# The last expert block summed by one-hot products, and the combination and norm put behind the expert loop without a barrier

## Chip, cores and metric

The kernel runs on one core of one Trainium2 chip. The metric is the device time in microseconds (us) of one execution; below, "span" is the time from the first to the last instruction in a profiled execution. The engines are TensorE (PE; its weight loads are shown as PEld), VectorE (DVE), ScalarE (ACT), GpSimd (POOL) and SyncE (SP), which issues most of the DMAs.

## Reference

Two transformer blocks are computed for 512 tokens of width 1024. What matters here is the end of the second block: a mixture of 32 experts with 4 experts for each token, and a layer norm behind it.

```python
def routed_experts(x, w_router, b_router, w_gate, b_gate, w_up, b_up, w_down, b_down):
    logits = (xt @ w_router + b_router).astype(jnp.float32)
    top_vals, top_idx = lax.top_k(logits, TOP_K)
    gates = jax.nn.softmax(top_vals, axis=-1).astype(x.dtype)
    ...
    def expert_block(args):
        xb, e = args
        gt = jnp.minimum(xb @ w_gate[e] + b_gate[e], SWIGLU_LIMIT)
        up = jnp.clip(xb @ w_up[e] + b_up[e], -SWIGLU_LIMIT, SWIGLU_LIMIT)
        hid = gt * jax.nn.sigmoid(SWIGLU_ALPHA * gt) * (up + 1.0)
        return hid @ w_down[e] + b_down[e]
    ...
    out = jnp.zeros((T + 1, D), x.dtype).at[row_tok].add(y_rows * row_gate[:, None])[:T]
...
        x = layer_norm(DEEPNORM_ALPHA * h + ffn, ln2_g[l], ln2_b[l])
```

## The kernel before

The last part of the kernel is three stages. Each stage ends with its semaphores cleared and a barrier of all engines (`Stage.__exit__`, lines 65 and 66), in front of which every engine drains.

The routing stage (`stage_mix_route`) ends with VectorE building a table, `c.slots`, that gives each row of each block its token and gate, and with GpSimd gathering the rows of block 0 by an indirect DMA (line 2501). VectorE then makes `ge`, the gates by token and expert, TensorE transposes it and ScalarE copies it to `c.geT` (line 2630). `c.bd` holds the 32 rows of the down bias.

The expert stage (`stage_experts`) runs blocks of 128 token-expert pairs, each with the weights of one expert. The loop has 24 turns of two blocks for at most 48; the routing of these inputs fills 33, numbered 0 to 32, and the turns left over are walked through by every engine with nothing in them. The weights of a block are 12 pieces of 1 MB. ScalarE rounds a piece to its high part (`high`, line 2965), VectorE subtracts for the low part (`low`, line 3024), and TensorE does three products for each tile (lines 2929 to 2931 and 2939 to 2941). The semaphore `w_low` counts the pieces, and with it SP loads the next weights. ScalarE and VectorE do the block's inputs (`x_part`) between two pieces; for block 0 they stand behind pieces 0 and 1. At the block's end ScalarE scales the result out of PSUM by the gate into `y` (line 3007), and GpSimd scatters `y` by token and rank to `pair_rows` in HBM (line 2874). GpSimd's order in block j is: gather the inputs of block j+1 (lines 2858 and 2861), wait for the result of block j, scatter it, wait until it has landed.

The last stage (`stage_combine_norm`) loads the four pair rows of each token (`r[:, m, k, :]`, 128 tokens for each m, 16 loads, line 3124), adds rows 1 to 3 and the bias product of `geT` and `bd` in PSUM by fp32 products (lines 3141 and 3145), adds row 0 and the residual on VectorE (lines 3171 and 3178), and does the norm with VectorE and ScalarE in turn (lines 3157 to 3193). The norm's gain and shift are spread over the partitions by products with a row of ones (line 3134).

## Time and profile before

| | |
|---|---|
| median of 3 runs | 3398.53 us (3397.7 to 3407.13) |
| the profiled execution | 3405.29 us, span 3403.5 us |
| mean granted TensorE clock in it | 0.966 |
| busy share of its span: PE, DVE, ACT, POOL | 93%, 78%, 53%, 22% |
| HBM traffic over the span | 255 GB/s |

Three views matter: the timeline of each engine in the last 110 us and around the start of the expert stage, the chain of work that ended last, and the waits within the expert loop. In the timelines a row has its start, its length, engine, line and operation, and in brackets how long the engine had been idle and what ended that.

### The profile page before, as it was taken

Reading aid. Unit: us, or ns where it says so; the run is one execution under the profiler, and the core shown is the slowest. Engines: PE = TensorE matmul, PEld = TensorE weight load, DVE = VectorE, ACT = ScalarE, POOL = GpSimd, SP = SyncE. Lnnn points to the kernel's source line nnn. Section 1 sums busy time; section 2 is a strip of 40 time slices with the busy share of each in tenths; the row PEclk is TensorE's granted clock in tenths of the full one; section 3 lists DMA queues with packets and bytes.
Section 4 is the critical chain, followed back from the end, with each engine's and each line's share of the span. In section 5 each row is a group of like instructions: output and inputs, shape, how many; then the busy total and the mean of one; then the engine's idle time right before and its main releaser. Section 6 shows DMA issues by size and latency. Waiting matters only on the chain. (4 is left out here: it accounts for less than half of the span.)

```text
span 3403.5 us, 47918 instructions
## 1 busy us (share of the span) xinstructions
PE 3159.8 (93%) x16448; PEld 2722.8 (80%) x16448; DVE 2669.1 (78%) x3821; ACT 1818.5 (53%) x2212; POOL 742.7 (22%) x459
## 2 busy tenths in 40 slices
PE   7999788999887999999998957999999999999996
PEld 7996677999887888888887846787888887887883
DVE  6885652994596788788788554999999999998993
ACT  4432443334584333333333342787777877777872
POOL 0000002545212454445454000011111111110110
PEclk9999789999998999999999978999999999999997
DMA  5221032334447899999997122999999999998983
GB/s 144 71 75 38 1 124 69 133 118 170 184 199 285 327 358 338 331 354 333 353 339 278 76 80 109 346 360 356 358 365 356 357 368 361 360 371 343 359 338 128
DMA packets 195371, 851.96 MB, mean 250 GB/s; under 512 B 21714, under 2 KB 104274, under 8 KB 151556
## 3 DMA queue, kind: packets, MB, share of 16 engines
q1 hardware_dynamic: 167332, 699.56, 56.1%
q0 software_dynamic: 27936, 151.02, 10.9%
q8 instruction: 65, 1.06, 0.1%
q14 instruction: 38, 0.31, 0.0%
HBM read 809.09 MB, written 59.24 MB: 255 GB/s over the span
## 5 line engine op out<-in xcount | busy, mean ns | idle before, releaser
L3024 DVE TENSOR_TENSOR moe_w_lo<-all_raw,moe_w_hi 128x2048 fp32r<-128x2048 f32 x298 | 676.8, 2288 | 61.5 <-ACT moe_w_hi L2965 59.1
L2965 ACT ACTIVATE moe_w_hi<-all_raw 128x2048 fp32r<-128x2048 f32 x298 | 568.4, 1915 | 80.8 <-PE moe_GU L2931 61.4
L2931 PE MATMUL moe_GU<-moe_w_hi,moe_x_lo 128*128 128x512 f32 x1056 | 412.1, 390 | 0.0
L2930 PE MATMUL moe_GU<-moe_w_lo,moe_x_hi 128*128 128x512 f32 x1056 | 411.9, 390 | 0.0
L2929 PE MATMUL moe_GU<-moe_w_hi,moe_x_hi 128*128 128x512 f32 x1056 | 411.5, 390 | 0.0
L1230 POOL TENSOR_TENSOR score_w_lo<-all_hT,score_w_hi 128x1024 fp32r<-128x1024 f32 x67 | 165.3, 2469 | 670.8 <-DVE all_x_lo L1346 530.6
L1855 DVE SCALAR_TENSOR_TENSOR experts_pair<-experts_pair,all_x_first 128x1024 f32<-128x1024 f32 x128 | 156.4, 1222 | 138.9 <-DMA experts_pair<-in_peer_pairs,experts_slot 138.9
L1699 POOL DMA_INDIRECT experts_pair<-in_peer_pairs,experts_slot x128 | 228.1, 1782 | 114.7 <-POOL experts_slot L1696 110.1
L2930 PEld LDWEIGHTS moe_GU<-moe_w_lo,moe_x_hi 128*128 128x128 f32 x1056 | 198.5, 188 | 42.1
L2931 PEld LDWEIGHTS moe_GU<-moe_w_hi,moe_x_lo 128*128 128x128 f32 x1056 | 198.5, 188 | 41.5
L2929 PEld LDWEIGHTS moe_GU<-moe_w_hi,moe_x_hi 128*128 128x128 f32 x1056 | 198.8, 188 | 40.5
L1696 POOL COPY experts_slot<-all_pair_id 128x1 uint32 x128 | 152.5, 1191 | 325.2 <-DVE all_h L1867 295.5
L3024 DVE TENSOR_TENSOR moe_w_lo<-all_hT,moe_w_hi 128x2048 fp32r<-128x2048 f32 x98 | 223.0, 2284 | 0.1
L2939 PE MATMUL moe_Y<-moe_w_hi,moe_hid_hi 128*128 128x512 f32 x528 | 213.0, 403 | 0.8 <-DVE moe_hid_lo L3054 0.8
L2941 PE MATMUL moe_Y<-moe_w_hi,moe_hid_lo 128*128 128x512 f32 x528 | 206.9, 392 | 0.0
L2940 PE MATMUL moe_Y<-moe_w_lo,moe_hid_hi 128*128 128x512 f32 x528 | 206.4, 391 | 0.0
L2965 ACT ACTIVATE moe_w_hi<-all_hT 128x2048 fp32r<-128x2048 f32 x98 | 187.7, 1915 | 32.0 <-PE moe_GU L2931 18.7
L2874 POOL DMA_INDIRECT pair_rows<-all_mixT,all_slot x33 | 45.9, 1391 | 718.0 <-ACT all_mixT L3007 718.0
L1254 PE MATMUL score_H<-all_x_hi,score_w_hi 128*128 128x384 f32 (+1 forms) x544 | 189.3, 348 | 1.6 <-DVE all_x_lo L1346 1.6
L1715 PE MATMUL experts_H<-all_x_hi,experts_wd_hi 128*128 128x384 f32 x512 | 173.4, 339 | 16.8 <-DVE experts_wd_lo L1837 16.6
L1256 PE MATMUL score_H<-all_x_hi,score_w_lo 128*128 128x384 f32 (+1 forms) x544 | 188.9, 347 | 0.0
L1255 PE MATMUL score_H<-all_x_lo,score_w_hi 128*128 128x384 f32 (+1 forms) x544 | 188.8, 347 | 0.0
(505 smaller groups left out, 8057.0 us busy)
## 6 DMA issues: line engine op xcount, KB each, us to landing
all_raw<-in_w_moe SPq DMA_DIRECT2D x149, 2048.0 KB, 9.2
all_hT<-in_w_moe SPq DMA_DIRECT2D x49, 2048.0 KB, 9.2
all_hT<-in_peer_wdT SPq DMA_DIRECT2D x128, 512.0 KB, 12.8
all_wu<-in_peer_pairs SPq DMA_DIRECT2D x64, 1024.0 KB, 13.4
peer_gates<-gates_out SPq DMA_DIRECT2D x6, 4096.0 KB, 11.6
experts_gt<-peer_gates SPq DMA_DIRECT2D x32, 768.0 KB, 10.4
all_hT<-in_w_in SPq DMA_DIRECT2D x40, 512.0 KB, 4.0
all_hid<-peer_early SPq DMA_DIRECT2D x60, 192.0 KB, 5.9
```

Of the source, the lines that this page charges most:

```text
L1254: pe.matmul(out, left, c.x_hi[:, k, at:T], start=(k == 0), stop=False)
L1255: pe.matmul(out, left, c.x_lo[:, k, at:T], start=False, stop=False)
L1256: mm = pe.matmul(out, low, c.x_hi[:, k, at:T], start=False, stop=(k == KD - 1))
L1699: pool.indirect_dma_start(out=pair[:, v, :], out_offset=None, in_=a["peer_pairs"][:, :], in_offset=bass.IndirectOffsetOnAxis(ap=slot[:, n: ...
L2929: pe.matmul(out, x_hi[:, kx, :], hi[:, k, :], start=False, stop=False)
L2930: pe.matmul(out, x_hi[:, kx, :], lo[:, k, :], start=False, stop=False)
L2931: mm = pe.matmul(out, x_lo[:, kx, :], hi[:, k, :], start=False, stop=(kx == KD - 1))
L2939: pe.matmul(Y[:, b, :], hid_hi[:, h, :], hi[:, f, cols], start=(h == 0), stop=False)
L2940: pe.matmul(Y[:, b, :], hid_hi[:, h, :], lo[:, f, cols], start=False, stop=False)
L2941: mm = pe.matmul(Y[:, b, :], hid_lo[:, h, :], hi[:, f, cols], start=False, stop=(h == KD - 1))
L2965: act.activation(w_hi[p % RING][:], piece_of(r, p), ACT.Copy).then_inc(w_high, 1)
L3024: dve.tensor_tensor(w_lo[p % RING][:], piece_of(r, p), w_hi[p % RING][:].bitcast(F32), ALU.subtract).then_inc(w_low, 1)
```

## The change

- The last block's result isn't scattered. ScalarE writes it, scaled by its gate, as a high part and VectorE as a low part into weight buffers; VectorE compares each row's token with a count to make a one-hot matrix for each of the four groups of 128 tokens (`token_hot`); TensorE multiplies the two, and so adds each row to its token in PSUM.
- At the start of the expert stage GpSimd therefore writes zeros to the last block's places in `pair_rows` by a scatter, and waits for its landing before it gathers for block 1.
- The combination and norm stand behind the loop in the same stage, with no barrier between. Pair rows are loaded into the input, output and weight buffers of the loop: row 0 when the other scatters have landed, rows 1 to 3 when all weights are split. GpSimd adds row 2 to row 1, so that TensorE adds two rows for each token instead of three. Gain and shift come by broadcasting DMAs.
- The bias product takes one pass of three stacked parts (`geT` and `bd` of 96 rows, high, high and low) in place of an fp32 product. For that the routing stage loads `bd` three times and splits it, and makes `ge` before the table `c.slots` instead of behind it.
- For block 0, `x_part` stands behind piece 0, ahead of piece 1.

```diff
+                for i in range(3):
+                    sp.dma_start(bd_raw[EXPERTS * i:EXPERTS * i + EXPERTS, :], a["b_down_2"][0]).then_inc(bd_in, 16)
...
+                act.wait_ge(bd_in, 48)
+                act.activation(c.bd[:], bd_raw, ACT.Copy).then_inc(bd_high, 1)
...
+                dve.wait_ge(bd_high, 1)
+                step(dve.tensor_tensor(c.bd[lows, :], bd_raw[lows, :], c.bd[lows, :].bitcast(F32), ALU.subtract))
...
+                step(dve.tensor_tensor(hg, hot, flat_gate.unsqueeze(2).to_broadcast([P, ENTRIES, EXPERTS]), ALU.mult))
+                for m in range(M):
+                    ins = dve.tensor_reduce(ge[:, m, 0, :], hg[:, m * EK:(m + 1) * EK, :].rearrange("p k e -> p e k"),
+                                            AX.X, ALU.add)
+                step(ins)
+                dve.tensor_copy(ge[:, :, 1:3, :], ge[:, :, 0:1, :].to_broadcast([P, M, 2, EXPERTS])).then_inc(ge_ok, 1)
...
                 dve.wait_ge(table_ok, 1)
                 step(dve.tensor_scalar(c.slots[:, 0:NBLK, 1], table[:, 0, :], float(4 * ROWS), None, ALU.add))
...
-                step(dve.tensor_tensor(hg, hot, flat_gate.unsqueeze(2).to_broadcast([P, ENTRIES, EXPERTS]), ALU.mult))
-                for m in range(M):
-                    ins = dve.tensor_reduce(ge[:, m, :], hg[:, m * EK:(m + 1) * EK, :].rearrange("p k e -> p e k"),
-                                            AX.X, ALU.add)
-                ins.then_inc(ge_ok, 1)
-
-
-def stage_experts(nc, c, a):
+                dve.wait_ge(ge_high, 1)
+                ge_lo = slice(2 * EXPERTS, 3 * EXPERTS)
+                step(dve.tensor_tensor(c.geT[ge_lo, :, :], ge_rows[ge_lo, :].rearrange("e (m t) -> e m t", m=M),
+                                       c.geT[ge_lo, :, :].bitcast(F32), ALU.subtract))
...
+        def pair_row(m, k):
+
+            if k == 0:
+                return (xg, y)[m // 2][:, m % 2, :]
+            return raw[k - 1][:, m * D:(m + 1) * D]
+
+        def result(m):
+            return pair_row(m, 2)
+
+        def total(m, h):
+
+            if m < 2:
+                return GU[:, 2 * m + h, :]
+            if m == 2:
+                return X[:, h, :, :].rearrange("p k t -> p (k t)")
+            return Y[:, h, :]
...
+                sp.wait_ge(all_stored, 1)
+                sp.wait_ge(w_low, n * PIECES)
+                for m in range(M):
+                    sp.dma_start(pair_row(m, 0), pair_src[:, m, 0, :]).then_inc(loaded[m][0], 16)
+                sp.wait_ge(w_low, n * PIECES + STARTED)
+                for m in range(M):
+                    for k in range(1, EK):
+                        sp.dma_start(pair_row(m, k), pair_src[:, m, k, :]).then_inc(loaded[m][k], 16)
+                    if m == 0:
+                        sp.dma_start(gain, a["ln2_g_2"].to_broadcast([P, D])).then_inc(gain_in, 16)
+                        sp.dma_start(shift, a["ln2_b_2"].to_broadcast([P, D])).then_inc(gain_in, 16)
+                for m in range(M):
+                    sp.wait_ge(finished, m + 1)
+                    sp.dma_start(tokens(out)[:, m, :], result(m)).then_inc(saved, 16)
+                sp.wait_ge(saved, 16 * M)
...
+                pool.memset(y[:, 1, :], 0.0).then_inc(zero_ok, 1)
+                pool.tensor_copy(last[:], c.slots[:, ds(n - 1, 1), :].rearrange("p o w -> p (o w)")).then_inc(last_ok, 1)
+                pool.wait_ge(zero_ok, 1)
+                pool.wait_ge(last_ok, 1)
+                scatter(y[:, 1, :], last[:, 1:2]).then_inc(zeroed, 16)
+                pool.wait_ge(zeroed, 16)
...
-                        pool.wait_ge(y_ok, j + 2)
-                        pool.sem_inc(paced, 1)
-                        pool.indirect_dma_start(out=c.pair_rows[:, :],
-                                                out_offset=bass.IndirectOffsetOnAxis(ap=slot[:, u, 1:2].bitcast(U32), axis=0),
-                                                in_=y[:, u, :], in_offset=None, bounds_check=ROWS - 1,
-                                                oob_is_err=False).then_inc(stored, 16)
-                        pool.wait_ge(stored, j * 16 + 16)
-                        pool.sem_inc(paced, 1)
+                            pool.wait_ge(y_ok, j + 2)
+                            pool.sem_inc(paced, 1)
+                            scatter(y[:, u, :], slot[:, u, 1:2]).then_inc(stored, 16)
+                            pool.wait_ge(stored, j * 16 + 16)
+                            pool.sem_inc(paced, 1)
...
+                pool.sem_inc(all_stored, 1)
+                for m in range(M):
+                    pool.wait_ge(loaded[m][1], 16)
+                    pool.wait_ge(loaded[m][2], 16)
+                    pool.tensor_tensor(pair_row(m, 1), pair_row(m, 1), pair_row(m, 2), ALU.add).then_inc(paired, 1)
+                    pool.wait_ge(paired, m + 1)
...
+                def bias_sums(m):
+                    for h in range(2):
+                        pe.matmul(total(m, h), c.geT[:, m, :], c.bd[:, h * CHUNK:(h + 1) * CHUNK], start=True, stop=False)
+
+                def last_block(m):
+                    for h in range(2):
+                        pe.matmul(total(m, h), token_hot[:, m, :], last_hi[:, h * CHUNK:(h + 1) * CHUNK], start=False, stop=False)
+                        pe.matmul(total(m, h), token_hot[:, m, :], last_lo[:, h * CHUNK:(h + 1) * CHUNK], start=False, stop=False)
+
+                for m in range(3):
+                    bias_sums(m)
+                pe.wait_ge(hot_ok, 1)
+                pe.wait_ge(last_low, 2)
+                for m in range(3):
+                    last_block(m)
+                bias_sums(3)
+                last_block(3)
+                for m in range(M):
+                    pe.wait_ge(loaded[m][3], 16)
+                    for h in range(2):
+                        pe.matmul(total(m, h), c.ident[:], pair_row(m, 3)[:, h * CHUNK:(h + 1) * CHUNK], start=False, stop=False)
+                    pe.wait_ge(paired, m + 1)
+                    for h in range(2):
+                        mm = pe.matmul(total(m, h), c.ident[:], pair_row(m, 1)[:, h * CHUNK:(h + 1) * CHUNK],
+                                       start=False, stop=True)
+                    mm.then_inc(folded, 1)
...
-                for p in range(2):
-                    high(0, 0, p, first=True)
+                high(0, 0, 0, first=True)
                 x_part(0)
-                for p in range(2, RING):
+                for p in range(1, RING):
...
-                        act.wait_ge(piece_done, j * PIECES + PIECES)
-                        for b in range(2):
-                            ins = act.activation(y[:, u, b * CHUNK:(b + 1) * CHUNK], Y[:, b, :], ACT.Copy,
-                                                 scale=slot[:, u, 2:3].bitcast(F32))
-                        ins.then_inc(y_ok, 1)
+                            act.wait_ge(piece_done, j * PIECES + PIECES)
...
+                act.activation(warm[:], c.ones[:, 0:1], ACT.Sqrt)
+                act.wait_ge(last_ok, 1)
+                act.wait_ge(piece_done, n * PIECES)
+                for b in range(2):
+                    act.activation(last_hi[:, b * CHUNK:(b + 1) * CHUNK], Y[:, b, :], ACT.Copy,
+                                   scale=last_gate).then_inc(last_high, 1)
...
-                dve.wait_ge(gain_ok, 2)
+                dve.wait_ge(last_ok, 1)
+                step(dve.tensor_copy(token[:, 0:1], last[:, 0:1]))
+                for m in range(1, M):
+                    ins = dve.tensor_scalar(token[:, m:m + 1], token[:, 0:1], float(-P * m), None, ALU.add)
+                step(ins)
+                for m in range(M):
+                    ins = dve.tensor_scalar(token_hot[:, m, :], c.count[:], token[:, m:m + 1], None, ALU.is_equal)
+                ins.then_inc(hot_ok, 1)
                 for m in range(M):
                     first_row(m)
+                for b in range(2):
+                    cols = slice(b * CHUNK, (b + 1) * CHUNK)
+                    dve.wait_ge(last_high, b + 1)
+                    dve.scalar_tensor_tensor(out=last_lo[:, cols], in0=Y[:, b, :], scalar=last_gate,
+                                             in1=last_hi[:, cols].bitcast(F32), op0=ALU.mult,
+                                             op1=ALU.subtract).then_inc(last_low, 1)
+                dve.wait_ge(gain_in, 32)
+                for m in range(M):
                     other_rows(m)
                     if m >= 1:
                         scale(m - 1)
                     centre(m)
                 scale(M - 1)
```

What moves on the engines shows at three places. First VectorE at the end of the routing stage, where `route_own` is the reduction of line 2742, `route_bb` and `route_ge` are the gates' product and sums, and `all_slots` is the table that the gather of block 0 reads. Before:

```order
L2742 TENSOR_REDUCE route_own<-route_ecmp 128x1
L2745 TENSOR_SCALAR all_slots<-route_acc 128x48
L2746 COPY all_slots<-route_acc 128x48
L2747 TENSOR_SCALAR all_slots<-all_slots 128x48
L2749 CAST all_owner<-route_end 1x1
L2751 TENSOR_SCALAR all_owner<-route_acc 1x48
L2752 TENSOR_TENSOR route_bb<-route_bb,route_gate 128x512
L2754 TENSOR_REDUCE route_ge<-route_bb 128x32 x4
```

With the change:

```order
L2748 TENSOR_REDUCE route_own<-route_ecmp 128x1
L2749 TENSOR_TENSOR route_bb<-route_bb,route_gate 128x512
L2751 TENSOR_REDUCE route_ge<-route_bb 128x32 x4
L2754 COPY route_ge<-route_ge 128x4x64
L2757 TENSOR_SCALAR all_slots<-route_acc 128x48
L2758 COPY all_slots<-route_acc 128x48
L2759 TENSOR_SCALAR all_slots<-all_slots 128x48
L2761 CAST all_owner<-route_end 1x1
L2763 TENSOR_SCALAR all_owner<-route_acc 1x48
L2766 TENSOR_TENSOR all_geT<-route_acc,all_geT 32x512
```

The product, the four sums and a new copy have moved ahead of the table.

Second, VectorE behind the loop, from the first instruction to the second group's sum. Before, behind the barrier:

```order
L3171 SCALAR_TENSOR_TENSOR all_h<-all_h,comb_r 128x1024
L3178 TENSOR_TENSOR all_h<-all_h,comb_ps 128x1024
L3182 TENSOR_SCALAR comb_mean<-comb_mean 128x1
L3184 SCALAR_TENSOR_TENSOR comb_r<-all_h,comb_mean,comb_gain 128x1024
L3171 SCALAR_TENSOR_TENSOR all_h<-all_h,comb_r 128x1024
L3178 TENSOR_TENSOR all_h<-all_h,comb_ps 128x1024
```

With the change, right behind the loop's last branch:

```order
L3247 CAST moe_token<-moe_last 128x1
L3249 TENSOR_SCALAR moe_token<-moe_token 128x1 x3
L3252 TENSOR_SCALAR moe_token_hot<-all_count,moe_token 128x128 x4
L3221 SCALAR_TENSOR_TENSOR all_h<-all_h,all_mixT 128x1024 x4
L3259 SCALAR_TENSOR_TENSOR moe_w_lo<-moe_Y,moe_last,moe_w_hi 128x512 x2
L3228 TENSOR_TENSOR all_h<-all_h,moe_GU 128x1024
```

All four additions of row 0 now stand ahead of the last block's low part (line 3259), and that ahead of the first sum.

Third, TensorE behind the loop, where `moe_GU`, `moe_X` and `moe_Y` are the PSUM sums of groups 0 and 1, 2, and 3. The last group of rows before:

```order
L3141 MATMUL comb_ps<-all_bd,all_geT 128x512 x2
L3145 MATMUL comb_ps<-comb_r,all_ident 128x512 x6
L3116 UNCONDITIONAL_BRANCH
```

The end with the change:

```order
L3039 MATMUL moe_Y<-all_bd,all_geT 128x512 x2
L3043 MATMUL moe_Y<-moe_w_hi,moe_token_hot 128x512
L3044 MATMUL moe_Y<-moe_w_lo,moe_token_hot 128x512
L3043 MATMUL moe_Y<-moe_w_hi,moe_token_hot 128x512
L3044 MATMUL moe_Y<-moe_w_lo,moe_token_hot 128x512
L3057 MATMUL moe_GU<-all_raw,all_ident 128x512 x2
L3060 MATMUL moe_GU<-all_raw,all_ident 128x512 x2
L3057 MATMUL moe_GU<-all_raw,all_ident 128x512 x2
L3060 MATMUL moe_GU<-all_raw,all_ident 128x512 x2
```

A group's six fp32 products have become four, and the products of the last block's rows stand ahead of all of them.

## Rows read from the trace of the kernel before

**Rows 1.** The page: its first line
```profile
span 3403.5 us, 47918 instructions
```

**Rows 2.** Who waited for whom (total us, times, longest us), 2165 to 3290 us
```profile
POOL all_slot L2858 <- DMA pair_rows<-all_mixT,all_slot: 312.9, 31, 12.2
...
PEld moe_X L2896 <- DMA all_mixT<-h_rows,all_slot: 16.4, 10, 4.3
```

**Rows 3.** Timeline of GpSimd, 3240 us to the end
```profile
3303.98 1.18 POOL L2874 DMA_INDIRECT pair_rows<-all_mixT,all_slot  x1 [21.18 <-ACT all_mixT L3007]
3338.38 0.97 POOL L2874 DMA_INDIRECT pair_rows<-all_mixT,all_slot  x1 [33.22 <-ACT all_mixT L3007]
```

**Rows 4.** Timeline of ScalarE, 3290 us to the end
```profile
3336.22 1.27 ACT L3007 ACTIVATE all_mixT<-moe_Y,all_slot 128x512 f32<-128x512 f32 x2 [7.36 <-PE moe_Y L2941]
```

**Rows 5.** Line 2819, the end of the expert stage (duration ns, start us)
```profile
L2819 DVEq DRAIN  x1: 17/17/17, 3334.7 to 3334.7; - x1
...
L2819 POOLq DRAIN  x1: 5373/5373/5373, 3345.2 to 3345.2; - x1
```

**Rows 6.** The chain that ended last, in order of time (start us, us)
```profile
3353.35 7.19 PE comb_wide L3134 x8
...
3363.95 7.72 PE comb_ps L3145 x12
...
3373.59 5.35 PE comb_ps L3145 x12
```

**Rows 7.** Timeline of VectorE, 3290 us to the end
```profile
3327.43 2.29 DVE L3024 TENSOR_TENSOR moe_w_lo<-all_raw,moe_w_hi 128x2048 fp32r<-128x2048 f32 x1
...
3371.72 1.22 DVE L3178 TENSOR_TENSOR all_h<-all_h,comb_ps 128x1024 f32<-128x1024 f32 x1 [7.94 <-PE comb_ps L3145]
...
3375.66 1.23 DVE L3171 SCALAR_TENSOR_TENSOR all_h<-all_h,comb_r 128x1024 f32<-128x1024 f32 x1
3378.97 1.22 DVE L3178 TENSOR_TENSOR all_h<-all_h,comb_ps 128x1024 f32<-128x1024 f32 x1 [2.08 <-PE comb_ps L3145]
...
3383.43 1.22 DVE L3171 SCALAR_TENSOR_TENSOR all_h<-all_h,comb_r 128x1024 f32<-128x1024 f32 x1
...
3393.49 1.22 DVE L3178 TENSOR_TENSOR all_h<-all_h,comb_ps 128x1024 f32<-128x1024 f32 x1 [1.57 <-PE comb_ps L3145]
```

**Rows 8.** Windows: PE, PEld, DVE, ACT, POOL busy, PEclk, DMA share, GB/s
```profile
3341.40:3344.80 3.40, 0.00 (x0) 0.00 (x0) 0.00 (x0) 0.00 (x0) 0.00 (x0) 0.50 0.00 0
```

**Rows 9.** Line 3124, the loads of pair rows, and their time to landing
```profile
L3124 SPq DMA_DIRECT2D comb_r<-pair_rows x16: 358/473/1053, 3352.0 to 3361.1; - x16
...
DMA to landing us min/median/max: 4.0/11.0/14.8
```

**Rows 10.** Timeline of VectorE, 627 to 645 us
```profile
628.29 2.96 DVE L1422 TENSOR_TENSOR score_place<-score_posf 128x128 bf16<-128x128 f32 x1
```

**Rows 11.** Timeline of GpSimd, 627 to 645 us
```profile
628.26 2.40 POOL L1230 TENSOR_TENSOR score_w_lo<-all_hT,score_w_hi 128x1024 fp32r<-128x1024 f32 x1 [3.04 <-ACT score_w_hi L1289]
```

**Rows 12.** Timeline of TensorE, 3300 to 3301 us, two neighbours
```profile
3300.28 0.39 PE L2930 MATMUL moe_GU<-moe_w_lo,moe_x_hi 128*128 128x512 f32 x1
3300.51 0.39 PE L2931 MATMUL moe_GU<-moe_w_hi,moe_x_lo 128*128 128x512 f32 x1
```

**Rows 13.** Timeline of VectorE, end of the routing stage and start of the experts
```profile
2116.89 0.22 DVE L2745 TENSOR_SCALAR all_slots<-route_acc 128x48 int32<-128x48 f32 x1 [1.61 <-PE route_acc L2573]
...
2117.65 0.71 DVE L2752 TENSOR_TENSOR route_bb<-route_bb,route_gate 128x512 f32<-128x512 f32 x1
2118.39 1.19 DVE L2754 TENSOR_REDUCE route_ge<-route_bb 128x32 f32<-128x128 f32 x4
...
2127.47 4.49 DVE L3024 TENSOR_TENSOR moe_w_lo<-all_raw,moe_w_hi 128x2048 fp32r<-128x2048 f32 x2 [0.75 <-ACT moe_w_hi L2965]
```

**Rows 14.** Line 2456, the end of the routing stage
```profile
L2456 POOLq DRAIN  x1: 4671/4671/4671, 2118.7 to 2118.7; - x1
```

**Rows 15.** Timeline of TensorE, the same stretch
```profile
2133.29 0.79 PE L2926 MATMUL moe_GU<-all_bias,moe_pick 128*128 128x512 f32 x1 [5.70 <-DVE moe_x_lo L3030]
```

143 lines of the change are left out of this document (57 added, 86 removed).

## The prediction

> **What bounds the kernel now.** I read the page's span first [rows 1], then the chain that ended last, then the timelines of its engines. The chain holds only the last stage: it starts at the barrier behind the expert loop and runs over TensorE, 7.19 us in the products that spread gain and shift and 5.35 us in each group's six fp32 products, to VectorE's last norm steps [rows 6]. So what counts is how long it takes from the last block's final product to the end. That product ends at 3336.2, where ScalarE starts on its result [rows 4]; to 3403.5 it is 67.3 us. The stretch divides in three: 14.4 us to 3350.6, where a drain of 5.37 us behind GpSimd's last scatter (3338.4 [rows 3]) ends and lets the barrier go [rows 5]; 21.1 us to the first sum on VectorE (3371.72); and 31.8 us of sums, norms and stores [rows 7].
>
> In the loop the engine that waits is TensorE, for the gathered inputs, in a third of the blocks: 16.4 us on its weight-load side in ten of them [rows 2]. Else it is full, one pass each 0.23 us [rows 12].
>
> **The change part by part, in the times of this execution.**
>
> *Start of the loop.* The routing stage's barrier waits for GpSimd's drain, 4.67 us from 2118.7 [rows 14], and that follows the gather, which follows the table. VectorE now does the gates' product, four sums and a copy before the table. Product and sums took 0.71 and 1.19 us; the copy of 256 elements I estimate at 0.35 us. Of these 2.25 us, 1.61 us fall in the idle time before the table [rows 13]: +0.6 us for all engines. Against it, `x_part` is one piece earlier: TensorE's first product waited for `moe_x_lo` until 2133.29 [rows 15], behind two low parts of together 4.49 us [rows 13]; one of them, 2.2 us, now comes later. First product: 1.6 us earlier. As its first piece then runs partly at the slow clock, I count 1.1 us of gain; bounds 0.6 us of loss and 1.6 of gain. The split of `bd` in the routing stage is hidden by the output projection's last products on TensorE, for which ScalarE and VectorE both wait; without that cover it is about 2.3 us, two operations on 1024 columns, of which VectorE's take 1.22 [rows 7].
>
> *The zero scatter.* GpSimd gathers for block 1 only when it has landed. By the 10.1 us that a landing costs a wait in the loop (312.9 over 31) [rows 2], and by estimate 4 us of clearing and issue, the gather goes out some 14 us after the loop's start (by estimate just ahead of VectorE's low part at 2127.5 [rows 13]) instead of at once, and lands 10 us later, near 2151; TensorE wants it when ten of block 0's twelve pieces are done, and it starts on the first at 2133 [rows 15], with over 140 passes of 0.23 in a block: near 2162. Nothing; should it be late, microsecond for microsecond. Its half megabyte lies beside weights that TensorE doesn't wait for.
>
> *The tail: what VectorE has ahead of the last low part.* It leaves the loop at 3334.7 [rows 5]. Then eight small operations on tokens, 1.4 us by estimate (0.1 to 0.3 each, like the 0.22 of a 128x48 one [rows 13]); four additions of row 0, 1.22 each [rows 7], which overlap by some 0.08: 4.6 us; two low parts of 128x512 from PSUM, 1.3 us. Row 0 is there in time: the scatter at 3303.98 [rows 3] lands near 3314, the loads follow near 3318, and no weight is in flight. ScalarE's high parts, 1.27 us from 3336.22 [rows 4], end before. So the low parts are ready at 3342.0.
>
> *GpSimd's additions.* SP may load rows 1 to 3 when the last piece is split, at 3329.7 [rows 7]. The first of 16 such loads landed after 4.0 us; the last, issued at 3361.1, after 14.8 [rows 9]: about 1.33 us for each after the first. So group 0's rows 1 and 2 are there at 3335.1, group 1's, sixth and seventh in the queue, at 3341.7, group 3's row 3, the fourteenth, at 3351. What GpSimd's two-input operation does to VectorE shows at 628: a 128x128 tensor-tensor took 2.96 us [rows 10] while GpSimd's 128x1024 ran for 2.40 from almost the same moment [rows 11]; it went on when GpSimd had ended. So the first addition, at 3335.1, stops VectorE for some 2.3 us: 3344.3. The second arrives at 3341.7 while VectorE is still at row 0 of the last groups; whether it gets in between two of these is open, so half of 2.3 us: 3345.4. Bounds 0 and 4.6. The Trainium skill (GPSIMD Engine Reference, 4.1 Engine selection) says that elementwise additions belong on VectorE, GpSimd being about twice as slow. By that rule this move loses; with them on VectorE the sum would be 4.6 us more there and no stall, 1.2 us worse than with them on GpSimd, and the rule is outweighed by which engine is waited for.
>
> *TensorE.* 18 passes for the last block and the last bias, 0.23 each [rows 12]: 4.1 us. Group 0's four fp32 products, two thirds of 5.35 [rows 6]: 3.6 us. First sum at 3353.1 at the full clock. But TensorE has stood nearly idle since 3336.2, save 1.4 us of bias products. In the trace of before the granted clock is 0.50 from 5.2 us after that time on [rows 8], the 1.2 GHz level, and group 0's products, partly under it, took 7.72 us in place of 5.35 [rows 6]. I take those 2.4 us: 3355.5. Bounds 0 and 4.8.
>
> *VectorE's chain.* With TensorE at 3.6 us a group, VectorE sets the pace: group 0 takes 3.9 us (3371.72 to 3375.66), the next two 4.46 each (3378.97 to 3383.43), then from the last sum 10.0 us to the end of the span (3393.49 to 3403.5) [rows 7, 1]. Last sum 3368.3, end 3378.3. Loads don't bind: group 3's rows are added by 3353.
>
> *The sum.* 3378.3 less 1.1 at the start is 3377.2, 26.3 us under 3403.5. The profiled execution lies some 7 us over the median of the runs, 3398.5; the same 26.3 taken from that median gives 3372.2. All bounds at their good end (1.3 us more at the start's 1.6 less 1.1, no stall, full clock) give 3370.9 for the span, 32.6 less; all at the bad end (4.6 stall, 4.8 clock, 0.6 lost at the start) 3382.5, 21 less.
>
> **The rivals.**
> 1. *The tail stays at the slow clock.* For it: the clock had fallen within 9 us of the last block's product [rows 8]. Against: it came back while group 0's products ran, which took 7.72 us where a later group's take 5.35 [rows 6]. All 18 passes and 16 fp32 products at half rate take 8.2 + 28.6 us from 3345.4: last sum 3382.2, end 3392.2, 3391.1 with the start's gain, 12.4 less: 3386. The Trainium skill (TensorE: Matmul & The Clock Gate, Part 1) says that the slow clock is the default state and activity releases it; by it the time would be this one only if the waits between groups count as idleness. Chance 0.07.
> 2. *The loads bind.* The two broadcasts of 512 KB for gain and shift stand in the queue ahead of groups 1 to 3. If each took 5 us instead of 1.3, group 3 would land at 3358.5 and be added by 3361, with its products at 3364.6: still ahead of the 3368.3 above. Only beyond that does each microsecond count once; 6 more give 3378. Chance 0.05.
> 3. *The loop gets slower, and the kernel with it.* Within a block GpSimd waits for a scatter's landing, copies the slots, gathers and lets that land, and ten of 31 gathers are late already [rows 2]. With GpSimd's waits put inside the inner branch and another buffer layout, a trip that is 1.2 us longer makes all 31 late: 37 us, and the kernel is slower by over 10 us, near 3410; at 2 us 3434. Against it: the same instructions, in the same order, in each trip. Chance 0.03.
> 4. *The gain is eaten within 0.3%,* by rivals 1 and 3 in part, or because the stage's end waits on GpSimd's drain again: its last indirect DMA is then long past, so I see no ground. Chance 0.03.
>
> **How the numbers follow.** The forecast has 0.82. A measurement tells 0.3% (10 us) from no change. Its own range is 21 to 32.6 us less, 3366 to 3378; executions of before spread from 3397.7 to 3407, late gathers by chance, which widens it to 3362 to 3382, and I stop there: rival 1 with 3386, and the slower one, are the part left out. Faster by over 0.3%: 0.82 + 0.07 + 0.05 = 0.94; within: 0.03; slower: 0.03.
>
> **What would show it.** Right: no gap of 14 us behind the last block's product; the last low part ends 7 to 11 us after VectorE leaves the loop, with one or two of the four row-0 additions or a token operation lengthened to 2.3 us or more while GpSimd adds; sums of VectorE 3.9 to 4.5 us apart; the last sum about 10 us before the end; first product of block 0 1 to 2 us earlier after the routing table. Wrong: sums 7 us apart (rival 1), TensorE waiting for loads (2), more late gathers (3). The prediction fails most easily in VectorE's 7.3 us ahead of the low parts, where order and stalls decide.

## The result and the profile after

The changed kernel took 3384.41 us (median of 8 runs, 3371.67 to 3407.19); the kernel before, run beside it, 3407.22 us (8 runs, 3396.92 to 3414.31). The ratio is 0.9941, with an interval of 0.9919 to 0.9963: between 13 and 28 us less. The forecast was 26.3 us less and 3372 us, with a range up to 3382; the time lies 2.4 us above it.

The page of the changed kernel's profiled execution, its first line:

```profile
span 3405.5 us, 47872 instructions
```

This execution is the slowest of the eight and 2 us longer than that of before [rows 1]. So the trace shows the gain and what ate it at once. I read it in four stretches, the marks being VectorE's `route_own` reduction (the last operation that both kernels have at the same place), TensorE's first bias product of block 0, and ScalarE's first scaling of the last block's result:

| stretch (us) | before | after | difference |
|---|---|---|---|
| up to `route_own` | 2115.1 | 2122.3 | +7.3 |
| from there to the first product | 18.2 | 16.6 | -1.6 |
| the loop | 1202.9 | 1226.2 | +23.2 |
| last block's result to the end | 67.3 | 40.4 | -26.9 |
| span | 3403.5 | 3405.5 | +2.0 |

**The end.** ScalarE's timeline in the changed kernel, then VectorE's:

```profile
3365.07 1.26 ACT L3129 ACTIVATE moe_w_hi<-moe_Y,moe_last 128x512 fp32r<-128x512 f32 x2 [1.84 <-PE moe_Y L3024]
```

```profile
3363.55 0.15 DVE L3247 CAST moe_token<-moe_last 128x1 f32<-128x1 int32 x1 [4.37 <-issue]
...
3364.05 3.06 DVE L3252 TENSOR_SCALAR moe_token_hot<-all_count,moe_token 128x128 fp32r<-128x128 f32 x4
3367.03 4.62 DVE L3221 SCALAR_TENSOR_TENSOR all_h<-all_h,all_mixT 128x1024 f32<-128x1024 f32 x4
3371.57 1.40 DVE L3259 SCALAR_TENSOR_TENSOR moe_w_lo<-moe_Y,moe_last,moe_w_hi 128x512 fp32r<-128x512 f32 x2
3382.36 1.22 DVE L3228 TENSOR_TENSOR all_h<-all_h,moe_GU 128x1024 f32<-128x1024 f32 x1 [9.40 <-issue]
...
3386.30 1.22 DVE L3228 TENSOR_TENSOR all_h<-all_h,moe_GU 128x1024 f32<-128x1024 f32 x1
...
3390.76 1.22 DVE L3228 TENSOR_TENSOR all_h<-all_h,moe_X 128x1024 f32<-128x1024 f32 x1
...
3395.22 1.22 DVE L3228 TENSOR_TENSOR all_h<-all_h,moe_Y 128x1024 f32<-128x1024 f32 x1
```

The mark of before is ScalarE's 3336.22 [rows 4], and of after 3365.07. GpSimd's timeline beside it:

```profile
3364.07 2.36 POOL L2966 TENSOR_TENSOR all_raw<-all_raw 128x1024 f32<-128x1024 f32 x1 [30.04 <-DMA all_raw<-pair_rows]
3370.93 2.93 POOL L2966 TENSOR_TENSOR all_raw<-all_raw 128x1024 f32<-128x1024 f32 x1 [4.49 <-DMA all_raw<-pair_rows]
```

and rows of TensorE's: the first and two more of the one-hot passes, one of those at full clock, and the first four of the passes of group 0's fp32 products:

```profile
3373.11 0.76 PE L3043 MATMUL moe_GU<-moe_w_hi,moe_token_hot 128*128 128x512 f32 x1 [4.96 <-DVE moe_w_lo L3259]
...
3374.10 0.63 PE L3043 MATMUL moe_GU<-moe_w_hi,moe_token_hot 128*128 128x512 f32 x1
3374.53 0.63 PE L3044 MATMUL moe_GU<-moe_w_lo,moe_token_hot 128*128 128x512 f32 x1
...
3376.33 0.40 PE L3043 MATMUL moe_X<-moe_w_hi,moe_token_hot 128*128 128x512 f32 x1
...
3378.67 1.88 PE L3057 MATMUL moe_GU<-all_raw,all_ident 128*128 128x512 f32 x4
```

The gap of 14 us is gone. Behind the mark the last low part ends at 7.9 us (9.2 forecast), the first sum starts at 17.3 (19.3), the last at 30.2 (32.1), and the span ends at 40.4 (42.1). The sums follow each other at 3.9, 4.5 and 4.5 us, so VectorE sets the pace. The four one-hot rows show the stall: they start with GpSimd's first addition, at 3364.05 and 3364.07, and take 3.06 us, 2.47 of them the first row alone. GpSimd's second addition was itself held (2.93 us instead of 2.36), and VectorE's low parts weren't. The first passes on TensorE come 0.43 us apart (3374.10, 3374.53), later ones 0.23.

**The start.** The two rows of VectorE's `route_own`, before and after, and the table's first row after; then TensorE's first product after, which answers to [rows 15]:

```profile
2115.09 0.19 DVE L2742 TENSOR_REDUCE route_own<-route_ecmp 128x1 f32<-128x32 f32 x1
```

```profile
2122.34 0.18 DVE L2748 TENSOR_REDUCE route_own<-route_ecmp 128x1 f32<-128x32 f32 x1
...
2124.62 0.22 DVE L2757 TENSOR_SCALAR all_slots<-route_acc 128x48 int32<-128x48 f32 x1
```

```profile
2138.91 0.79 PE L3009 MATMUL moe_GU<-all_bias,moe_pick 128*128 128x512 f32 x1 [3.65 <-DVE moe_x_lo L3154]
```

18.2 us have become 16.6, 1.6 less, as forecast for the first product.

**What ate it.** The granted clock in the attention stage and in the loop (start:end, us, then PE, PEld, DVE, ACT and POOL busy, PEclk, DMA share, GB/s), before and after:

```profile
1965.00:2045.00 80.00, 48.38 (x312) 34.28 (x313) 52.03 (x108) 36.57 (x104) 1.73 (x5) 0.77 0.28 96
2150.00:3320.00 1170.00, 1151.11 (x5274) 944.89 (x5273) 1105.02 (x803) 908.78 (x675) 152.88 (x94) 1.00 0.93 357
```

```profile
1965.00:2045.00 80.00, 45.14 (x288) 32.80 (x289) 45.57 (x104) 34.47 (x103) 1.72 (x5) 0.66 0.18 65
2150.00:3320.00 1170.00, 1136.80 (x5179) 932.47 (x5177) 1090.63 (x794) 892.54 (x662) 150.66 (x93) 0.99 0.93 354
3317.90:3324.70 6.80, 4.59 (x15) 4.01 (x16) 2.37 (x3) 2.58 (x3) 0.00 (x0) 0.50 0.71 286
```

The code of the attention stage is the same in both. Its short products leave TensorE waiting often, and the granted clock averaged 0.77 in one execution and 0.66 in the other: 8.8 us of full clock in 80. The changed kernel was 1.4 us late ahead of this stage and 7.3 behind it, so some 6 of the 7.3 us of the table's first row arose here, beside the lower clock; no run changes the clock alone. In the loop the cause is in the waits, of the changed kernel and then of the one before (total us, times, longest us):

```profile
POOL all_slot L2925 <- DMA pair_rows<-all_mixT,all_slot: 322.4, 31, 13.7
...
PE moe_X L2979 <- DMA all_mixT<-h_rows,all_slot: 28.3, 14, 4.5
```

```profile
PE moe_X L2896 <- DMA all_mixT<-h_rows,all_slot: 13.8, 11, 3.8
```

TensorE waited 28.3 us for gathered inputs, against 13.8 in the trace of before. The longest wait, step by step on GpSimd and then TensorE:

```profile
3290.53 1.52 POOL L2934 DMA_INDIRECT pair_rows<-all_mixT,all_slot  x1 [21.47 <-ACT all_mixT L3116]
3304.19 1.62 POOL L2925 COPY all_slot<-all_slots 128x3 int32 x1 [12.14 <-DMA pair_rows<-all_mixT,all_slot]
3306.67 3.00 POOL L2928 DMA_INDIRECT all_mixT<-h_rows,all_slot  x1 [0.85 <-POOL all_slot L2925]
```

```profile
3320.11 1.97 PE L2979 MATMUL moe_X<-all_ident,all_mixT 128*128 128x128 f32 x8 [4.49 <-DMA all_mixT<-h_rows,all_slot]
```

The scatter left at 3290.53 and had landed only when the copy could start, 13.7 us later; copy and issue took 2.5, and the gathered rows were there 13.4 us after the issue: 29.6 us in all, 4.5 more than there was room for. 2.3 us into the wait of 4.49 us the clock fell to its half level, and stayed there for 6.8 us, which is the last of the rows of windows above. In the trace's record of the clock the half level held for 27.3 us inside the changed kernel's loop and for 6.8 in that of before; 4.4 and 1.0 us of that lay within waits, where it cost nothing, and half of the rest was lost: 11.4 and 2.9 us. 14.5 us more of waits and 8.5 more of clock make 23.0 of the loop's 23.2.

### The profile page after: what moved, and what is told of

Read it like the earlier page. It is cut to its first block and busy times, and to the rows that moved or that the text cites. A ratio compares the mean times of both kernels' runs of the same rounds, so it can differ in the third digit from the quotient of the medians.

```text
span 3405.5 us, 47872 instructions
## 1 busy us (share of the span) xinstructions
PE 3155.6 (93%) x16432; PEld 2732.6 (80%) x16432; DVE 2677.4 (79%) x3834; ACT 1822.1 (54%) x2211; POOL 750.4 (22%) x465
## 6 DMA issues: line engine op xcount, KB each, us to landing
all_wu<-in_peer_pairs SPq DMA_DIRECT2D x64, 1024.0 KB, 13.8
```

## Experiments

Three questions: is the gain what I summed, why is the time higher, and were the terms at the end the right ones? "Mark" is from here on ScalarE's first scaling of the last block's result, and "loop" and "end" are the last two stretches of the table above.

### The same kernels again

`before_again` and `after_again` are the two kernels unchanged.

> The kernel before, unchanged, for a second trace. In the first, TensorE waited for gathered inputs in 11 of the loop's blocks, 13.8 us, and lost 3.4 us more to the half clock inside the loop; the changed kernel's trace shows 14 waits, 28.3 us, and 13.7 us of clock. Theory A (the loop is the same in both kernels and only scatters from execution to execution): this trace shows another sum, anywhere in 10 to 40 us for the two together. Theory B (the change made the loop slower): this one stays near 17 us and that of after_again near 42.

Measured: 3397.72 us, one run. TensorE waited 7.6 us for gathers, seven times, and the clock was full in the loop behind its first 4 us; the end took 66.7 us.

> The changed kernel, unchanged, for a second trace and a second set of times. Theory A: the stretch from the last block's product to the end is again 40 to 41 us against 67 before, the loop's waits and clock loss differ from the first trace's 42 us, and the median lies 20 to 28 us under before. Theory B: loop loss again near 42 us, median 12 to 20 us under before.

Measured: 3382.0 us (6 runs, 3377.79 to 3390.0) against 3402.53 of before (17 runs), ratio 0.9936 (0.9915 to 0.9958). The end took 41.0 us, the waits 19.1 us. Theory A holds for the end; for the loop, two traces of each decide nothing.

### Gathers that don't wait for a scatter's landing

In both kernels GpSimd's next gather stands behind the landing of the last scatter, since both take their indices from one small table. The edit gives the scatter a table of its own (`place`), and moves the wait:

```diff
                             gather(j + 1, 1 - u)
+                            pool.wait_ge(stored, j * 16 + 16)
+                            pool.sem_inc(paced, 1)
+                            pool.tensor_copy(place[:, 1 - u, :], c.slots[:, ds(j + 1, 1), :].rearrange("p o w -> p (o w)")).then_inc(placed, 1)
                         pool.wait_ge(y_ok, j + 2)
...
-                                                out_offset=bass.IndirectOffsetOnAxis(ap=slot[:, u, 1:2].bitcast(U32), axis=0),
+                                                out_offset=bass.IndirectOffsetOnAxis(ap=place[:, u, 1:2].bitcast(U32), axis=0),
...
-                        pool.wait_ge(stored, j * 16 + 16)
...
+                        act.wait_ge(placed, j + 1)
```

> The kernel before, with the wait for a scatter's landing moved from ahead of the next gather to ahead of the next scatter, and a second small table so that the two don't share one. The gather is issued some 11 us earlier. If late gathers (scatter landing 11.5 us, then copy and issue 3, then landing 12) are what scatters the loop, TensorE waits for no gather, the half clock is gone from the loop, the loop falls from 1202.9 to about 1186 us, the median falls by 17 to 25 us and the spread of the runs shrinks to that of the attention stage, some 8 us. If the gathers queue behind the scatter anyway: no change.

> The same edit on the changed kernel. Theory A: loop 1186 us here too, and the difference of medians to before_free is the pure gain of the change: 1.6 us at the loop's start and 26.9 us at the end, 28.5 us; my prediction's own sum is 26.3. Theory B: the loop stays 5 us or more longer than that of before_free, and the difference is 20 to 23 us.

Measured: `before_free` 3398.31 us (12 runs, 3393.28 to 3404.69), ratio 0.9986 (0.9973 to 0.9999); `after_free` 3370.29 (6 runs, 3367.18 to 3375.34), 0.99 (0.9882 to 0.9919). TensorE waited for no gather in either, and the clock was full behind the loop's first 5 us, yet the loop took 1199.7 and 1199.5 us, not 1186. Each block took 36.3 us where one without a wait took 35.9 before. Two bias products that stand 25 passes apart in a block, in `before_free`:

```profile
2502.53 0.39 PE L2933 MATMUL moe_GU<-all_bias,moe_pick 128*128 128x512 f32 x1
...
2508.36 0.39 PE L2933 MATMUL moe_GU<-all_bias,moe_pick 128*128 128x512 f32 x1
```

They are 5.83 us apart. The small tables had been allocated ahead of `x_hi` and `x_lo`, which so lay 24 or 36 bytes further on in every partition, and with them all that is allocated behind them, `hid_hi` and `hid_lo` too. The next two kernels differ from these in that alone (`before_free2` is shown):

```diff
-        place = s.sb("place", [P, 2, 3], I32)
...
         x_hi = s.sb("x_hi", [P, KD, P], F32R)
...
         hid_lo = s.sb("hid_lo", [P, KD, P], F32R)
+        place = s.sb("place", [P, 2, 3], I32)
```

> As before_free, but with the two new small tables (24 and 12 bytes a partition) put behind x_hi, x_lo and the hidden tiles instead of ahead of them. In before_free and after_free TensorE waited for no gather, yet 24 of its passes took 5.60 us in place of 5.44, in every block. Theory A: the tables had moved the stationary tiles' addresses by 24 or 36 bytes, and that alone made each pass 2.9% longer; now 24 passes take 5.44 again, a block 35.9 us, the loop 1186 us, the median 14 us less than before_free's, near 3384. Theory B: passes are longer because TensorE never pauses; then 5.60 and 3398 again.

> The changed kernel with the same edit and the tables behind. Theory A: 5.44 us for 24 passes, loop 1186, median near 3357; the difference to before_free2 is the change's gain without the gathers' noise, 28.5 us by the traces (1.6 at the start, 26.9 at the end), 26.3 by my prediction. Theory B: 3370 again.

The same two products in `before_free2`:

```profile
2524.63 0.39 PE L2933 MATMUL moe_GU<-all_bias,moe_pick 128*128 128x512 f32 x1
...
2530.30 0.39 PE L2933 MATMUL moe_GU<-all_bias,moe_pick 128*128 128x512 f32 x1
```

5.67 us apart. Measured: `before_free2` 3388.81 us (7 runs), ratio 0.995 (0.9931 to 0.9968), loop 1186.4; `after_free2` 3360.61 (4 runs), 0.9875 (0.9853 to 0.9897), loop 1187.0. Theory A holds: the placing of the small tables had made the passes 2.8% longer, in all of the loop's products with weights (233 ns against 227 from one to the next on average), and the loop 13 us. Which of the shifted tiles does it wasn't tried. The passes alone would make 29 us (148 a block, 33 blocks, 5.9 ns each). The rest is hidden, since with short passes TensorE waits elsewhere, as `before_free2` shows by this wait, of which `before_free` has none:

```profile
PEld moe_GU L2910 <- DVE moe_hid L3057: 14.2, 31, 0.8
```

And the two loops are equal to 0.6 us. With 1186.4 and 1187.0 us as the loops without a late gather, the eleven traces of kernels whose passes are short and whose gathers are late can be added up: that, plus TensorE's waits for gathers, plus half of the time at the half clock outside these waits, gives every loop to within 1 us (1226.8 for 1226.2 in the changed kernel's first trace, 1203.1 for 1202.9 in that of before, 1207.9 for 1207.9 in `after_again`). So the loops of these traces differ by late gathers and the clock behind them, and by nothing else that is over 1 us. GpSimd's timeline in `before_free2`, scatter, copy, gather, and the copy for the next scatter:

```profile
2528.78 1.52 POOL L2882 DMA_INDIRECT pair_rows<-all_mixT,moe_place  x1 [20.14 <-ACT all_mixT L3015]
2530.30 1.77 POOL L2861 COPY all_slot<-all_slots 128x3 int32 x1
2532.93 2.73 POOL L2864 DMA_INDIRECT all_mixT<-h_rows,all_slot  x1 [0.85 <-POOL all_slot L2861]
2539.20 0.46 POOL L2879 COPY moe_place<-all_slots 128x3 int32 x1 [3.54 <-DMA pair_rows<-all_mixT,moe_place]
```

The gather goes out 4.2 us after the scatter. In this pair the change is worth 28.2 us by medians, 26.2 by means. Its traces give 24.5 at start and end (1.9 and 22.6): before_free2's end is 63.7 us, for the loop's empty turns now lie beside the last scatter's landing. One part of the expectation failed: the runs' spread did not shrink to 8 us. It is 11.4 us in `before_free` and 16.3 in `before_free2`, and 8.2 in the two changed ones. A part of the spread lies ahead of the loop: `route_own` starts anywhere from 2108.1 to 2122.3 us in the nineteen traces.

### Is the changed kernel's loop slower?

By these numbers gathers cost the kernel before some 15 us (3405.8 us, the mean of all its 106 runs here, less 3.5 for the empty turns and 3387.6) and the changed one, in its first 14 runs, some 23 (3384.5 less 3361.4). Does a part of the change do it? `before_zero` adds the zero scatter to the kernel before. `after_nest` takes the scatter out of the inner branch again, for all blocks, and leaves out the zero scatter and the one-hot products:

```diff
                         with pool.If(j + 1 < n):
                             gather(j + 1, 1 - u)
-                            pool.wait_ge(y_ok, j + 2)
-                            pool.sem_inc(paced, 1)
-                            scatter(y[:, u, :], slot[:, u, 1:2]).then_inc(stored, 16)
+                        pool.wait_ge(y_ok, j + 2)
+                        pool.sem_inc(paced, 1)
+                        scatter(y[:, u, :], slot[:, u, 1:2]).then_inc(stored, 16)
```

> The kernel before, plus the changed kernel's zero scatter at the start of the expert stage (the last block's places are written with zeros, and its own scatter overwrites them later). Two theories on why the changed kernel's loop lost 28.3 and 18.9 us to late gathers in two traces and the kernel before 13.8 and 7.6. Theory B1 (the zero scatter shifts GpSimd's queue for good): here too waits of 18 us or more, median 8 us over before. Theory A (nothing, or another part): 7 to 16 us, median within 3 us of before; block 1's gather not late.

> The changed kernel with the scatter of every block, the last too, standing outside GpSimd's and ScalarE's inner branch as before, no zero scatter and no one-hot products, and with the wait for each landing in its old place. Theory B2 (the waits inside the inner branch made the loop's gathers later): waits of 7 to 16 us in the loop, median near scatter_last's 3370 plus 13 for the gathers and 3.6 for the turns of the loop behind the last landing: 3387. Theory B3 (the layout or the rest of the changed kernel): waits of 18 us or more, median near 3397.

`before_x` has `x_part(0)` of ScalarE and VectorE behind piece 0, `before_route` the changed routing stage with `geT` and `bd` of 96 rows, `before_sems` only this:

```diff
+        spare = [s.sem(f"spare{i}") for i in range(36)]
         raw_in = [s.sem(f"raw_in{i}") for i in range(RAW)]
```

> The kernel before with one edit of the change: block 0's x_part behind piece 0. First product 1.6 to 2.2 us earlier. If this order is what makes later gathers late: TensorE waits 18 us or more for gathers in the trace, and the median is 6 to 8 us over before. If not: 7 to 15 us of waits, and 0 to 3 us under before.

> The kernel before with the changed kernel's routing stage (bias loaded three times and split, the gates' product and sums ahead of the table), and so one bias pass for each group's half in the last stage in place of an fp32 product: 1.91 us to about 0.5 for each of four groups, 5.5 us less at the end, 0.6 more at the start. If the routing stage makes the gathers late: waits of 18 us or more, and the median 2 to 4 us over before. If not: 7 to 15 us, and 4 to 6 us under before.

> The kernel before with 36 unused semaphores allocated ahead of those of the expert stage, so that raw_in and stored get about the numbers that they have in the changed kernel. If the numbers matter: waits of 18 us or more, median 8 us over before. If not (as I expect): as before.

and `before_route_x` has the edits of the first two; `after_third` is the changed kernel.

> The kernel before with the changed routing stage and block 0's x_part behind piece 0. By its parts 9.8 us under before (8.1 in the last stage, 1.7 at the start). If what runs ahead of the loop makes its gathers later: some 8 us of that is lost and the median lies 0 to 3 us under before. If it doesn't: 8 to 11 us under before, and the extra loss belongs to the changed kernel's loop or end.

> The changed kernel once more beside it. By its parts 28 us under before (26 at the end, 1.7 at the start). If the loop really loses more to late gathers in this kernel: 19 to 22 us under before, as in two sets of runs so far (19.7 and 20.1 by means). If those two sets were chance: 25 to 29 us.

All of them, in us. "By parts" is what the traces' starts and ends give against before; "measured" is the difference of the means of the runs, each against the runs of before beside it; with a standard error of 1.8 to 3.4 us in all rows but the first, where it is 4.8; the wait is TensorE's for gathers in the one trace:

| kernel | runs | median | ratio and interval | by parts | measured | wait |
|---|---|---|---|---|---|---|
| changed kernel | 8 | 3384.41 | 0.9941 (0.9919 to 0.9963) | -28 | -19.7 | 28.3 |
| after_again | 6 | 3382.0 | 0.9936 (0.9915 to 0.9958) | -28 | -20.1 | 19.1 |
| after_third | 6 | 3375.71 | 0.9909 (0.9887 to 0.9931) | -28 | -31.0 | 8.2 |
| after_nest | 12 | 3395.2 | 0.9976 (0.9959 to 0.9993) | -16 | -8.9 | 17.8 |
| before_zero | 12 | 3401.68 | 0.9989 (0.9975 to 1.0004) | 0 | -2.3 | 14.6 |
| before_x | 12 | 3404.38 | 0.9986 (0.9972 to 0.9999) | -2.4 | -3.7 | 17.3 |
| before_route | 12 | 3403.61 | 0.999 (0.9972 to 1.0009) | -7.5 | -2.8 | 16.6 |
| before_sems | 12 | 3409.9 | 1.0001 (0.9983 to 1.0019) | 0 | +1.1 | 17.4 |
| before_route_x | 12 | 3398.79 | 0.9974 (0.9957 to 0.9991) | -9.8 | -9.4 | 14.8 |

No single part is seen to make the loop slower, as far as standard errors of 2 to 3 us allow: `before_zero`, `before_x`, `before_sems` and `before_route_x` come out within 2.3 us of their parts; `before_route` alone was 4.7 off, and `before_route_x`, which contains it, 0.4. `after_nest` was 7 off with a wait of 17.8 us, so the nesting isn't the cause either: without it the loss was still there. Then `after_third` fell on the other side, 31 us less, as the theory of chance had it. Over its three sets the changed kernel has a mean of 3382.1 us (20 runs, one standard error 2.1), 23.7 under before, where 28 follow from the parts. Whether the missing 4 us are chance, or the changed loop loses a few more to late gathers, stays open; what is shown is that with the gathers out of the way both loops take the same time.

### The end, term by term

All of these are `after_free2` with one edit. Its end takes 41.1 us from the mark. `scatter_last` scatters the last block as the others and waits for the landing; the one-hot products are gone, and there is still no barrier:

```diff
-                pe.wait_ge(hot_ok, 1)
-                pe.wait_ge(last_low, 2)
-                for m in range(3):
-                    last_block(m)
+                pe.wait_ge(y_ok, n + 1)
                 bias_sums(3)
-                last_block(3)
```

> after_free2 without the one-hot products: the last block is scattered like the others and its landing waited for, the combination still follows without a barrier. It splits the gain. By rows: y 1.3, issue 0.9, landing 11.5, seven loads 12, GpSimd's addition 2.4, four fp32 products 3.4: first sum 31.5 us behind the last product; all 18 loads, addition and products: last sum 44.5, end 55 us behind it, against 67.3 before and 40.4 with the products. So 12 us for the barrier and 15 us for the one-hot products. If the barrier was nearly all of it (rival): under 45 us.

Its span, and GpSimd's timeline with the last scatter and the first addition:

```profile
span 3369.8 us, 47884 instructions
```

```profile
3322.75 0.99 POOL L2936 DMA_INDIRECT pair_rows<-all_mixT,moe_place  x1 [32.84 <-ACT all_mixT L3118]
3337.33 2.34 POOL L2971 TENSOR_TENSOR all_raw<-all_raw 128x1024 f32<-128x1024 f32 x1 [13.59 <-DMA all_raw<-pair_rows]
```

With its mark at 3320.60 the end takes 49.2 us, not 55: the landing was over in about 3.5 us instead of 11.5, with no weight in flight any more (the loads behind it go out from 3326.20). The last scatter of before had landed in 3.2 us too, where those within its loop took 9.3 to 13.4. The median is 3370.47 (4 runs), 0.9897 (0.9876 to 0.9918). So of 67.3 us, 18 go without the one-hot products, and 8 more with them; I had expected 12 and 15. The 18 aren't the barrier's alone: the moved wait gives 3.6, as in `before_free2`, and the bias products in one pass gave 8 in `before_route`, whose end took 58.9 us with the barrier in place (67.0 in the two traces of before). If the two add up here too, some 6 are left for the barrier, the drain, the staging and GpSimd's additions together, which no run separates.

`low_first` has VectorE's two low parts ahead of the row-0 additions:

```diff
-                for m in range(M):
-                    first_row(m)
                 for b in range(2):
...
+                for m in range(M):
+                    first_row(m)
```

> after_free2 with VectorE's two low parts ahead of the four row-0 additions. These took 4.62 us ahead of the low parts, while TensorE stood; behind them they lie beside TensorE's 9.4 us. Expected: low parts done 4.6 us earlier, first sum 4 to 4.6 us earlier, unless GpSimd's second and third addition (3373.9 and 3377.1 in the trace) become what the groups wait for; end 36 us behind the last product instead of 40.4. Rival (loads bind): group 3's rows, added at 3381, hold the last sum, gain under 2 us.

VectorE's timeline in it, the one-hot rows, the low parts, the first sum, the next norm operation and the last sum:

```profile
3319.06 2.98 DVE L3258 TENSOR_SCALAR moe_token_hot<-all_count,moe_token 128x128 fp32r<-128x128 f32 x4
3321.96 1.40 DVE L3263 SCALAR_TENSOR_TENSOR moe_w_lo<-moe_Y,moe_last,moe_w_hi 128x512 fp32r<-128x512 f32 x2
...
3331.46 1.22 DVE L3234 TENSOR_TENSOR all_h<-all_h,moe_GU 128x1024 f32<-128x1024 f32 x1 [3.57 <-issue]
...
3334.09 2.95 DVE L3240 SCALAR_TENSOR_TENSOR all_raw<-all_h,moe_mean,all_hT 128x1024 f32<-128x1024 f32 x1
...
3345.99 1.22 DVE L3234 TENSOR_TENSOR all_h<-all_h,moe_Y 128x1024 f32<-128x1024 f32 x1
```

The end takes 36.2 us from its mark at 3320.09, 5.0 less. TensorE stands only 0.3 us between the bias products and the one-hot ones, and its clock is full until the last sum, where `after_free2` had the half level for 6.8 us; so 1 us or so of the gain is clock. GpSimd's last addition now meets VectorE's norm (2.95 us in place of 1.28). The median is 3359.17 (4 runs), ratio 0.9866 (0.9845 to 0.9887), only 1.4 us under `after_free2`: the difference of two medians of four runs doesn't resolve 5 us here, the traces do.

`dve_pairs` puts GpSimd's additions on VectorE, behind the low parts:

```diff
-                    pool.tensor_tensor(pair_row(m, 1), pair_row(m, 1), pair_row(m, 2), ALU.add).then_inc(paired, 1)
...
+                    dve.tensor_tensor(pair_row(m, 1), pair_row(m, 1), pair_row(m, 2), ALU.add).then_inc(paired, 1)
```

> after_free2 with the additions of row 2 to row 1 on VectorE, behind the two low parts, in place of GpSimd. In after_free2 GpSimd's first addition stretched VectorE's four one-hot rows from some 0.7 to 3.04 us. Expected: no stretch, low parts 2.3 us earlier, the four additions of 1.22 us beside TensorE's one-hot passes; end 38.9 us behind the last product in place of 41.2. By my prediction's sum (additions on VectorE cost 1.2 us more than on GpSimd): 42.4. Rival: group 3's rows land at 13.8 us and VectorE, waiting for them, holds the first sum back: no gain.

VectorE's timeline, the one-hot rows, the low parts, the last of the additions and the first sum:

```profile
3319.81 0.88 DVE L3253 TENSOR_SCALAR moe_token_hot<-all_count,moe_token 128x128 fp32r<-128x128 f32 x4
...
3325.14 1.40 DVE L3260 SCALAR_TENSOR_TENSOR moe_w_lo<-moe_Y,moe_last,moe_w_hi 128x512 fp32r<-128x512 f32 x2
...
3334.78 1.23 DVE L3266 TENSOR_TENSOR all_raw<-all_raw 128x1024 f32<-128x1024 f32 x1 [2.61 <-DMA all_raw<-pair_rows]
3336.20 1.22 DVE L3229 TENSOR_TENSOR all_h<-all_h,moe_GU 128x1024 f32<-128x1024 f32 x1 [0.20 <-DVE all_raw L3266]
```

The one-hot rows take 0.88 us in place of 3.04, and the end 38.5 us, 2.6 less, close to the 38.9 expected. The last addition waited for its load and ended just ahead of the first sum. The median is 3362.35 (4 runs, of which one took 4563 us at a granted clock of 0.71; 3361.04 without it, and the ratio is 0.9873, 0.984 to 0.9906). The means of the other three and of `after_free2` are 3361.2 and 3361.4: the runs don't show the 2.6 us, which rest on one trace of each.

`best` has the low parts first, GpSimd's additions only for groups 0 and 1 and only behind the low parts, and a third fp32 product for groups 2 and 3:

```diff
+                pool.wait_ge(last_low, 2)
-                for m in range(M):
+                for m in range(2):
...
+                    if m >= 2:
+                        pe.matmul(total(m, h), c.ident[:], pair_row(m, 2)[:, h * CHUNK:(h + 1) * CHUNK], start=False, stop=False)
```

> after_free2 with low parts ahead of the row-0 additions, GpSimd's additions only for groups 0 and 1 and only once the low parts are done, and a third fp32 product on TensorE for groups 2 and 3. Expected: low parts 2.3 us earlier than in low_first (no addition beside them), first sum at 9.2 us behind the last product, sums 3.9, 4.5 and 4.5 us apart, no stretched operation of 2.95 us among them; end 32 us behind the last product against 36.3 in low_first, median near 3355. Rival (two additions of GpSimd now collide with the sums): 35 us or more.

VectorE's timeline and GpSimd's:

```profile
3322.34 0.88 DVE L3265 TENSOR_SCALAR moe_token_hot<-all_count,moe_token 128x128 fp32r<-128x128 f32 x4
...
3325.43 8.98 DVE L3234 SCALAR_TENSOR_TENSOR all_h<-all_h,all_mixT 128x1024 f32<-128x1024 f32 x4
3334.34 1.21 DVE L3241 TENSOR_TENSOR all_h<-all_h,moe_GU 128x1024 f32<-128x1024 f32 x1
...
3347.91 1.22 DVE L3241 TENSOR_TENSOR all_h<-all_h,moe_Y 128x1024 f32<-128x1024 f32 x1 [0.73 <-PE moe_Y L3072]
```

```profile
3325.60 3.30 POOL L2972 TENSOR_TENSOR all_raw<-all_raw 128x1024 f32<-128x1024 f32 x1 [32.93 <-DVE moe_w_lo L3270]
3329.33 2.87 POOL L2972 TENSOR_TENSOR all_raw<-all_raw 128x1024 f32<-128x1024 f32 x1 [0.43 <-DMA all_raw<-pair_rows]
```

The end takes 34.8 us, nearly the rival's 35 and not the 32 expected. The one-hot rows are short, but the low parts then wait for ScalarE, and TensorE's bias products end only at the same time, so 1 us of the gain is lost; the two additions hold VectorE's four row-0 additions (8.98 us for 4.62), and the last sum waits 0.7 us for the third product. The median is 3354.6 (5 runs, 3353.85 to 3359.99), ratio 0.9855 (0.9833 to 0.9878): the fastest kernel of this study, some 49 us under before.

## Why the prediction was right and wrong

What the sum was about came out: 26.3 us less were forecast, and the medians side by side are 22.8 apart, the means of the changed kernel's twenty runs and of before's 106 are 23.7 apart, and the traces' starts and ends 28. What failed is where that sum was put.

- **What bounds the end**: right. The gap behind the last product, the barrier and the fp32 products were the path, and without them the end is 26.9 us shorter where 25.2 were summed (67.3 less 42.1).
- **VectorE ahead of the low parts**: 7.9 us where 9.2 were taken. Only one addition of GpSimd hit it, on the one-hot rows rather than on a row-0 addition; the half addition counted for the second didn't come, since that one was held itself. The mechanism of [rows 10, 11] is confirmed by `dve_pairs`.
- **GpSimd against VectorE**: wrong. I had VectorE's own additions 1.2 us dearer, thinking of them only ahead of the low parts, an order that no run has; behind the low parts they lie beside TensorE's work, and the end of `dve_pairs` is 2.6 us shorter in its trace. I had set the Trainium skill's rule (GPSIMD Engine Reference, 4.1 Engine selection) aside, that elementwise additions belong on VectorE. The rule holds in this order, and its own reason (GpSimd's addition is slower, 2.36 against 1.22 us) is in the rows; what decides is the stall. The Trainium skill (SBUF — State Buffer, "SBUF: two separate sides") calls the port that the two engines share an exclusive lock. The rows agree: who comes second waits for the other's whole operation, GpSimd too (2.93 us for 2.36), and where both start within 0.02 us it was VectorE that waited.
- **TensorE's slow clock**: a size. Six passes at 0.43 us and not 0.23 are 1.2 us; 2.4 were taken, for the fp32 products, which ran at the full clock. The rival in which the end stays at the slow clock didn't happen.
- **VectorE's chain and the loads**: right, 12.9 us from the first sum to the last for 12.8, and no sum waited for a load.
- **The start**: right in its parts, 1.6 us; 1.1 were counted, 0.5 being taken off for a slow clock. The zero scatter cost nothing: block 1 wasn't late in the changed kernel's trace.
- **The step that failed** is that from the sum to the time: "the profiled execution lies some 7 us over the median of the runs, 3398.5; the same 26.3 taken from that median gives 3372.2". 3398.5 was the median of three runs. Over 106 runs the kernel before has a mean of 3405.8 and a median of 3405.7, and the profiled 3405.3 was an ordinary execution. 3405.7 less 26.3 is 3379.4; the changed kernel's 20 runs have a median of 3381.2. That lies just inside the range: the base was 7 us low, and that the first eight runs came out 2.4 us beyond the range and not within it was chance (the standard error of their mean is 4 us).
- **The range** failed with it. I gave the spread of before 3397.7 to 3407, and let it widen the range by 4 us on each side. But an execution can lose from 8 to 40 us in the loop alone (waits plus clock), and executions are up to 14 us apart when they come to it, some 6 of them from the attention stage: before ranged from 3393 to 3423, the changed kernel from 3367 to 3407. The loop's part was to be seen in one trace: ten late gathers of up to 4.3 us and one half-clock stretch behind the longest. The "1.3 us more" that the lower bound names for the start is 0.5; its sum, 3370.9, has the 0.5. The third rival, a loop made slower by over 37 us, didn't happen; a loop slower by a few us isn't excluded.
